# Norms of a two-model block kernel: one VectorE operation per tile, the shift on ScalarE, the order of the backlog around them

## The reference

```
# first model, per layer
mod = silu(c) @ ada_w[i] + ada_b[i]              # shift, scale, gate (one set for x, one for the context)
h = x * (1.0 + scale) + shift
...                                              # layer 0: attention, layer 1: S5
x = layer_norm(alpha * x + gate * ((y * silu(z)) @ w_out[i]), ln_g[i], ln_b[i])

# second model, per layer
hl = rms_norm(xl, norm_mix) * (1.0 + sc1_l) + sh1_l
...                                              # attention, mLSTM, pooling from hl @ w_in
xl = xl + g1_l * (concat @ w_out)
h2l = rms_norm(xl, norm_ffn) * (1.0 + sc2_l) + sh2_l
xl = xl + g2_l * ((silu(h2l @ w_g) * (h2l @ w_u)) @ w_d)
```

## Time and profile before

| | us |
|---|---|
| median of 3 runs | 2583.42 (2580.16 to 2589.23) |
| the profiled execution | 2589.86 |
| its span on the core | 2588.1 |

### The profile page before, as it was taken

The page is one execution under the profiler, slowest core; times in us unless marked ns, Lnnn a source line. Parts: engine busy times, 40 slices in busy tenths (PEclk is TensorE's granted clock), DMA queues, the critical chain, the costliest instruction groups (busy, mean ns, idle before and its releaser), DMA issues.

```text
span 2588.1 us, 33786 instructions
## 1 busy us (share of the span) xinstructions
PE 2212.1 (85%) x13593; PEld 1669.5 (65%) x13593; DVE 1360.2 (53%) x2527; ACT 906.5 (35%) x1779; POOL 504.7 (20%) x457
## 2 busy tenths in 40 slices
PE   6979788869899776489898988779999987977998
PEld 5757566558466565389753444558888855546998
DVE  4548677563446999155443356453333333455554
ACT  3234454551212432154222244232222222344443
POOL 0047878420057950000000011000000000000000
PEclk8989899889899988599898988889999998998999
DMA  8254454643444329975541211332323332315553
GB/s 281 72 176 132 133 149 121 214 132 99 134 107 107 86 67 180 248 205 166 177 124 57 91 57 50 114 100 96 98 88 90 106 109 76 104 49 163 186 164 106
DMA packets 423666, 324.38 MB, mean 125 GB/s; under 512 B 65086, under 2 KB 411470, under 8 KB 422358
## 3 DMA queue, kind: packets, MB, share of 16 engines
q1 hardware_dynamic: 386452, 295.70, 39.2%
q10 hardware_dynamic: 34242, 16.92, 2.3%
q0 software_dynamic: 2816, 9.60, 1.1%
HBM read 292.42 MB, written 29.75 MB: 124 GB/s over the span
## 4 chain that ended last, share of the span: by engine, by line
PE 61%; DVE 13%; POOL 9%; ACT 6%; DMA 5%; issue 4%; SPq 1%; ACTq 1%; DVEq 0%; POOLq 0%
PE ps L119 59%; POOL A L88 8%; ACT A L115 3%; DVE A L88 2%; DMA wbuf<-ctab 2%; DVE R L88 2%; PE ps L122 2%; DVE A L102 2%; DVE A L92 1%; DVE A L105 1%; SPq L125 1%; DVE A L93 1%; DMA wbuf<-in_ada_w 1%; POOL A L125 1%; DVE A L96 1%
## 5 line engine op out<-in xcount | busy, mean ns | idle before, releaser
L119 PE MATMUL ps<-R,R 128*128 128x256 f32 (+1 forms) x3968 | 845.2, 335 | 35.3 <-ACT R L115 25.1
L119 PEld LDWEIGHTS ps<-R,R 128*128 128x128 f32 x3968 | 631.5, 193 | 109.6 <-ACT R L115 30.3
L119 PE MATMUL ps<-HR,R 128*128 128x512 f32 (+1 forms) x1984 | 555.3, 364 | 35.6 <-DVE R L88 24.8
L88 DVE TENSOR_TENSOR R<-wbuf,R 128x1024 fp32r<-128x1024 f32 (+2 forms) x304 | 332.2, 1101 | 376.3 <-ACT R L115 376.1
L115 ACT ACTIVATE A<-ps 128x512 f32<-128x512 f32 (+4 forms) x400 | 210.4, 556 | 613.4 <-PE ps L119 410.1
L119 PEld LDWEIGHTS ps<-HR,R 128*128 128x128 f32 x1984 | 357.1, 193 | 94.4 <-issue 28.6
L88 POOL TENSOR_TENSOR A<-A 128x512 f32<-128x512 f32 (+3 forms) x258 | 294.6, 1156 | 527.0 <-DVE A L96 267.0
L88 DVE TENSOR_TENSOR A<-A 128x128 f32<-128x128 f32 (+4 forms) x796 | 359.6, 482 | 62.8 <-ACT A L115 25.9
L115 ACT ACTIVATE R<-wbuf 128x1024 fp32r<-128x1024 f32 (+2 forms) x304 | 270.0, 894 | 291.1 <-PE ps L119 264.0
L119 PE MATMUL ps<-H,wbuf 128*128 128x512 f32 (+2 forms) x928 | 342.0, 527 | 13.8 <-DVE H L93 13.8
L119 PE MATMUL ps<-A 128*128 128x64 f32 (+10 forms) x1736 | 285.2, 364 | 34.6 <-DMA wbuf<-ctab 9.4
(11 more groups left out here) (102 smaller groups left out, 1624.5 us busy)
## 6 DMA issues: line engine op xcount, KB each, us to landing
wbuf<-in_w_ada SPq DMA_DIRECT2D x48, 1024.0 KB, 5.2
wbuf<-in_ada_w SPq DMA_DIRECT2D x24, 1024.0 KB, 9.7
wbuf<-in_w_out SPq DMA_DIRECT2D x24, 1024.0 KB, 5.6
wbuf<-in_w_ffn_gate SPq DMA_DIRECT2D x22, 1024.0 KB, 5.3
wbuf<-in_w_ffn_up SPq DMA_DIRECT2D x22, 1024.0 KB, 5.7
wbuf<-in_w_ffn_down SPq DMA_DIRECT2D x32, 704.0 KB, 4.7
wbuf<-in_attn_w_in SPq DMA_DIRECT2D x20, 1024.0 KB, 6.8
ctab<-A ACTq DMA_DIRECT2D x64, 256.0 KB, 2.8
```

Source lines behind the costliest of these rows:

```text
L88: return self.op(lambda e: e.tensor_tensor(out, a, b, op))
L119: return self.op(lambda e: e.matmul(out, lhsT, rhs, start=start, stop=stop, skip_group_check=True))
```

## The change

In `LayerNorm` the two operations per k-tile become one scalar_tensor_tensor (X times g times root). For LN1 the beta is folded into `Mod2`: a few small column operations (`columns`) give the shift of H and of alpha times X. For LN2 ScalarE adds beta, in a third piece of the stage, and the backlog steps around it are split 2, 2, 3. In `RmsMod` VectorE does X times column times root, and `act2` adds the shift on ScalarE, behind the square root. For rm2 (`RmsModHalves`) ScalarE writes the high half with the shift, and VectorE makes the low half of k-tile k - 1 behind the root operation of k-tile k; the FFN waits per k-tile. `ffn` gets `prime`: two high halves and one low half of its weights, made before the root, and its two first panels are loaded two backlog panels earlier. In layer 1 the last two backlog steps go ahead of the mixer's output.

```diff
 # Lin3
+    def sp ... if self.prime:
+                    for g in self.grs[0:2]:
+                        load(g)
+                    yield
+    def act ... if self.prime:
+                    for n in (1, 2):
+                        self.act_hi(act, next(ahead))
+                    yield
+    def lows ... if self.prime:
+                    self.make_lo(e, next(ahead), s)
+                    n = 1
+                    yield
 # LayerNorm
                 rsqrt_act(act, self.RS[:, self.c0:512], (self.name, "rs"))
+                yield
+                for k in range(8 if self.bcol else 0):
+                    act.wait_ge(dve_step, (self.name, "g", k))
+                    act.act(X[:, k, self.c0:512], X[:, k, self.c0:512], ACT.Identity, bias=self.bcol(k)
+                            ).then_inc(act_step, (self.name, k))
                 for k in range(8):
-                    dve.tt(X[:, k, c0:512], X[:, k, c0:512], self.RS[:, c0:512], MUL).then_inc(dve_step)
-                    dve.wait_own()
-                    dve.ts(X[:, k, c0:512], X[:, k, c0:512], self.g(k), self.bcol(k), MUL, ADD
-                           ).then_inc(dve_step, (self.name, k))
+                    dve.stt(X[:, k, c0:512], X[:, k, c0:512], self.g(k), self.RS[:, c0:512], MUL, MUL
+                            ).then_inc(dve_step, (self.name, "g", k))
 # Mod2
+            def columns(self, dve):
+                M = MODS[1]
+                dve.wait_ge(act_evac, ("ada1", "t", 7))
+                dve.ts(self.AB, self.B, ALPHA, None, MUL).then_inc(dve_step)
+                for s in range(2):
+                    dve.tt(self.BH[:, s], M[:, 8:16, s], self.B, MUL).then_inc(dve_step)
+                dve.wait_own()
+                for s in range(2):
+                    dve.tt(self.BH[:, s], self.BH[:, s], M[:, 0:8, s], ADD).then_inc(dve_step)
 # flow, LN2
             step(ln)
             step(backlog, 2)
             step(ln)
-            step(backlog, 5)
+            step(backlog, 2)
+            step(ln)
+            step(backlog, 3)
 # RmsMod
             def act2(self, act):
                 rsqrt_act(act, RS[:, self.cc:512], (self.name, "rs"))
+                for k in range(8):
+                    self.shift(act, k)
...
                 for k in range(8):
-                    dve.tt(self.Hd[:, k, cc:512], X[:, k, cc:512], RS[:, cc:512], MUL).then_inc(dve_step)
-                    dve.wait_own()
-                    for s in range(cc // 256, 2):
-                        sl = slice(s * 256, s * 256 + 256)
-                        dve.ts(self.Hd[:, k, sl], self.Hd[:, k, sl], S1[:, k, s:s + 1], MOD[:, self.csh + k, s:s + 1],
-                               MUL, ADD).then_inc(dve_step, (name, k))
+                    for s, sl in self.kinds():
+                        dve.stt(self.Hd[:, k, sl], X[:, k, sl], S1[:, k, s:s + 1], RS[:, sl], MUL, MUL
+                                ).then_inc(dve_step, (name, k))
+                    between(k)
+            def shift(self, act, k):
+                act.wait_ge(dve_step, (self.name, k))
+                for s, sl in self.kinds():
+                    act.act(self.Hd[:, k, sl], self.Hd[:, k, sl], ACT.Identity, bias=MOD[:, self.csh + k, s:s + 1]
+                            ).then_inc(act_step, (self.name, "h", k))
+        class RmsModHalves(RmsMod):
+            def act2(self, act, first):
+                first()
+                rsqrt_act(act, RS[:, self.cc:512], (self.name, "rs"))
+                for k in range(8):
+                    act.wait_ge(dve_step, (self.name, k))
+                    for s, sl in self.kinds():
+                        act.act(HHf[:, k, sl], self.Hd[:, k, sl], ACT.Identity, bias=MOD[:, self.csh + k, s:s + 1]
+                                ).then_inc(act_hi, (self.name, "hi", k))
+            def lo(self, dve, k):
+                dve.wait_ge(act_hi, (self.name, "hi", k))
+                for s, sl in self.kinds():
+                    dve.stt(HLf[:, k, sl], self.Hd[:, k, sl], MOD[:, self.csh + k, s:s + 1], HHf[:, k, sl], ADD, SUB
+                            ).then_inc(dve_lo, (self.name, "lo", k))
 # layer flow
             on(LastHead(1))
-            step(backlog, 2)
+            if l:
+                rest(backlog)
+            else:
+                step(backlog, 2)
             e.mark(N + "mix")
...
             on(rm2)
-            on(second_half(rm2))
-            if l:
-                rest(backlog)
-            else:
-                step(backlog, 4)
+            ff = on(ffn)
             if e.name in ("act", "dve"):
                 e.wait_mark(N + "ff")
-            on(HalvesHT())
-            rest(on(ffn))
+            if e.name == "sp":
+                step(backlog, 2)
+                step(ff)
+                step(backlog, 2)
+            elif e.name == "act":
+                rm2.act2(e, lambda: step(ff))
+            elif e.name == "dve":
+                rm2.dve2(e, lambda: step(ff))
+            if e.name != "sp":
+                step(backlog, 4)
+            rest(ff)
```

More of the change, by code:

```diff
@@ L325, in build, with __init__ @@
         class Lin3:
-            def __init__(self, tiles, GR, gk=8, sub="dve", start=None, lead=0, fine=False):
+            def __init__(self, tiles, GR, gk=8, sub="dve", start=None, lead=0, fine=False, prime=False):
                 self.tiles, self.GR, self.sub, self.start, self.lead, self.fine = tiles, GR, sub, start, lead, fine
+                self.prime = prime
                 self.grs = []
@@ L348, in sp, with load @@
                 done = set()
+                def load(g):
+                    t, k0, kk, k1, nk, pk, width = g
+                    if pk not in done:
+                        done.add(pk)
+                        s = pool_step if self.sub == "pool" else dve_lo
+                        load_panel(sp, pk, t.w, k0, kk, pk[2], width, (s, self.end[pk]))
+                if self.prime:
+                    for g in self.grs[0:2]:
+                        load(g)
+                    yield
                 for j, t0 in enumerate(self.tiles):
                     for t in self.tiles[j:j + 1 + self.lead]:
-                        for _, k0, kk, k1, nk, pk, width in self.groups(t):
-                            if pk not in done:
-                                done.add(pk)
-                                s = pool_step if self.sub == "pool" else dve_lo
-                                load_panel(sp, pk, t.w, k0, kk, pk[2], width, (s, self.end[pk]))
+                        for g in self.groups(t):
+                            load(g)
                     for g in self.groups(t0):
@@ L427, in dve @@
                 lows = self.lows(dve, dve_lo) if self.sub == "dve" else None
+                if self.prime:
+                    next(lows)
+                    yield
                 for j, t in enumerate(self.tiles):
@@ L1189, in flow @@
             step(ln)
+            mod2 = Mod2()
+            if e.name == "dve":
+                mod2.columns(e)
             step(backlog, 4)
-            step(ln)
+            rest(ln)
             step(backlog, 4)
             e.mark("ln1")
-            on(Mod2())
+            on(mod2)
             SS.flow(e, on, backlog)
@@ L2157, in act2, with kinds, dve2 @@
                 rsqrt_act(act, RS[:, self.cc:512], (self.name, "rs"))
+                for k in range(8):
+                    self.shift(act, k)
             def dve(self, dve):
                 pass
-            def dve2(self, dve):
-                cc, name = self.cc, self.name
+            def kinds(self):
+                return [(s, slice(s * 256, s * 256 + 256)) for s in range(self.cc // 256, 2)]
+            def dve2(self, dve, between=lambda k: None):
+                cc, name, rs = self.cc, self.name, RS[:, self.cc:512]
@@ L2164, in dve2 @@
                 dve.wait_ge(mm_done, (name, "ss", 7))
-                rsqrt_dve(dve, RS[:, cc:512], PS[name, "ss"][:, cc:512], D, 1e-6, (name, "rs"))
+                dve.ts(rs, PS[name, "ss"][:, cc:512], 1.0 / D, 1e-6, MUL, ADD).then_inc(dve_evac, (name, "rs"))
+                between(-1)
+                dve.wait_ge(act_step, (name, "rs"))
+                dve.recip(rs, rs).then_inc(dve_step)
+                t = dve.own
                 dve.wait_ge(act_evac, self.mod)
+                S1 = self.S1
@@ new lines, in shift, with dve2, between @@
+            def shift(self, act, k):
[17 more added lines that the diff above has]
+                            ).then_inc(dve_lo, (self.name, "lo", k))
+            def dve2(self, dve, first):
+                def between(k):
+                    if k == -1:
+                        first()
+                    elif k:
+                        self.lo(dve, k - 1)
+                super().dve2(dve, between)
+                self.lo(dve, 7)
@@ L2185, in second_half @@
             return Second()
-        rm1 = RmsMod(N + "m1", 0, VT[:, 224 + 8 * l:232 + 8 * l], 8, 0, x_ready, H, (f"ada{2 + l}", "t", 7))
```

(15 more changed lines are left out.)

40 lines of the change are left out of this document (25 added, 15 removed).

## The result

| | before | after |
|---|---|---|
| median of the runs side by side | 2586.32 us (2580.16 to 2589.3, 4 runs) | 2610.8 us (2608.96 to 2619.09, 4 runs) |
| the profiled execution | 2589.86 | 2608.96 |
| its span on the core | 2588.1 | 2607.1 |
| mean granted clock | 0.914 | 0.909 |

The changed kernel is slower: the ratio is 1.0089, 95% interval 1.0063 to 1.0115. A second comparison, with more runs, gave 1.0070 (1.0045 to 1.0095). By the ratios the change costs 18 to 23 us, and the two profiled executions lie 19.1 us apart. Forecast were +12.2 us and a range up to 2609; the measured median of 2610.8 lies just outside of it. The sign was right and the sum too small.

A forecast was written before the change was run, and what follows sets the result against it. TensorE was taken to carry 61% of the chain, its backlog in lock-step with ScalarE's copies. Seven terms, -4.1 + 0.4 + 6.2 + 6.1 + 7.4 + 3.7 - 7.5 = +12.2, on 2583.4 gave 2595.6 us, range 2577 to 2609.

The forecast's parts named there:

- LN1: First norm, up to S5: eight scalar_tensor_tensor replace eight pairs of VectorE operations; -4.1 us (-3 to -4.3).
- LN2: TensorE waits for the seventh modulation panel, so halved VectorE work gains nothing; ScalarE's shifts delay copies; +0.4 us (0 to +1).
- rm1, layer 0: Backlog copies stand behind ScalarE's 16 shifts, stopping TensorE ahead of Keys; +6.2 us (+4 to +8.5).
- rm1, layer 1: Copies behind ScalarE's shifts again, with two whole backlog products still to do ahead of Keys; +7.4 us (+5 to +9).
- rm2, layer 0: Backlog held behind ScalarE's last shift, fourth backlog panel then loads late, FFN starts later; +6.1 us (+4 to +9).
- end of the mixer, layer 1: Last two backlog steps and a second turn go ahead of the mixer's output halves; +3.7 us (+3 to +4.5).
- rm2, layer 1: No backlog left to block; TensorE starts the FFN on the first low half of H; -7.5 us (-6 to -8.5).
- credit of 1.2 us: Layer 0's rm2: backlog products just done bring back 1.2 us of the FFN first tile's low clock.
- rival C: The forecast's mechanism at lower prices, clock back at once and panel sooner: +3 to +7 us; 12 in 100.
- rival B: Stalls of rm1 are given back later as weights arrive and head norms catch up: 2582.0 us, no change; 10 in 100.
- Rival A: Backlog stays hidden, ScalarE's copies do not hold TensorE for long: -21.5 us, 2561.9 us; 12 in 100.
- rival E: A second pass over two f32 SBUF inputs makes each 256-column operation 0.27 us longer: +26 us, 2621 us; 2 in 100.

The follow-up runs named there:

- experiment that kept TensorE busy: Changed kernel plus eleven 512-column TensorE products nobody reads, ahead of the backlog in rm1 of both layers; 2609.11 us, ratio 1.0054 to the kernel before.
- before again: The kernel before, executed once more without an edit for a second trace; 2584.74 us.
- the first model's norms alone: Kernel before with only the change to LayerNorm, Mod2, LN2's backlog split and the wait of layer 0's rm1 that follows; 2589.55 us, ratio 0.9999.
- rm1's order: Changed kernel with ScalarE doing its three backlog steps ahead of the sixteen shifts in rm1 of both layers; 2589.87 us, ratio 0.9982 to the kernel before.
- both orders: Changed kernel with ScalarE's backlog copies moved ahead in rm1 and between root and high halves in rm2; 2571.71 us, ratio 0.9924; again 2580.93 us, 0.9939.
- the last experiment: ScalarE's order mended in rm1 and rm2, and layer 1's last two backlog steps back in rm2 behind the root; 2569.06 us, ratio 0.9906 to the kernel before.

## Why the prediction was off

Step by step, in the terms of its sum:

| term | forecast | measured |
|---|---|---|
| LN1 | -4.1 | -4.2 (in the other traces with this code -4.2 to -5.7) |
| LN2 | +0.4 | +0.5 (-0.5 to +0.9 in the others) |
| rm1, layer 0 | +6.2 | **+8.7** (+8.8 again) |
| rm1, layer 1 | +7.4 | +7.6 (+7.7) |
| rm2, layer 0 | +6.1 | **+7.9** (+8.1) |
| end of the mixer, layer 1 | +3.7 | +3.5 |
| rm2, layer 1 | -7.5 | -7.0 |
| mixer of layer 1 | none | **+3.1** (+6.1) |
| the other stretches | 0 | -1.0 before LN1, +0.5 in S5, -0.6 elsewhere |
| sum | +12.2 | +19.1 |

**The step that failed is the size of what follows a stop of TensorE.** The sum took the low clock behind the restart to last 4.6 us and let the backlog's products pay a part of it. In rm1 of layer 0 it lasted 8.3 us, and the term of +6.2 measured +8.7; in rm2 of layer 0 the credit of 1.2 us did not come, and with a panel that was later by 0.4 the term of +6.1 measured +7.9. The seven terms add up to +17.0 where +12.2 was forecast. The stretches that the sum put at nothing gave 2 us more in this pair of executions.

**Behind the missed range stands also the base.** The +19.1 of the two profiles would have made 2602.5, which lies within the range. The other 8.3 us up to 2610.8 are the difference between profiles and medians: the forecast took differences within an execution of 2589.86 us and added them to a median of three runs that lies 6.4 us lower, and the profile after lies 1.8 us below its own median. The median of the kernel before was 2586.3 in the comparison side by side and 2593.9, 2589.7 and 2597.4 in the later ones. So the 2583.4 of three runs was itself a term that moves by several us, and the forecast gave it no range.

**The mechanism was right.** ScalarE's `mrow` copies stand behind its shifts and hold TensorE's backlog, and behind that Keys and the FFN. In layer 0, counted from the end of the sum of squares, the copy was forecast 12.5 us behind it and came at 12.4; Keys' first product was forecast at 16.1 and came at 16.6. In layer 1 that was 17.8 and 17.8. In rm2 of layer 0 the copy in question was to end 18.3 us behind the first backlog product and ended at 18.1, the last panel was to be there at 26.1 and was at 26.5, the FFN at 28.3 and was at 29.0. Undoing the order and nothing else took away these three terms and some 10 us more (in rm1 16.1 us in place of the 17.6 of the kernel before, twice, in rm2 12.3 in place of 21.0). The low bound of +4 for rm1, rival C, and rival B, that the stop is given back later, are out: the ratio lies at 0.7 to 0.9%, and the mixer of layer 0 is as long as before to 0.2 us.

**Two terms were too small, mainly by the clock, and one was missing.** First, rm1 of layer 0. The forecast took the low clock to last 4.6 us behind the restart, from the FFN in the earlier trace rows, and so gave Keys' first tile 7.4 us. The granted clock of the kernel after, by windows:

```profile
1312.00:1313.00 1.00, 0.76 (x4) 0.50 0.00 0
1313.00:1315.00 2.00, 2.00 (x18) 0.50 0.04 8
...
1320.00:1321.00 1.00, 1.00 (x3) 0.71 0.02 5
1321.00:1322.00 1.00, 1.00 (x4) 1.00 0.00 0
...
2120.00:2122.00 2.00, 2.00 (x25) 0.50 0.00 0
2122.00:2123.00 1.00, 1.00 (x14) 0.64 0.55 71
```

The clock is the third column from the right. Half clock (1.2 GHz of 2.4) from the restart at 1312.24 until about 1320.6, 8.3 us; the tile took 9.5 us. In layer 1, with one more whole product of the backlog behind the restart at 2118.43, the clock was back at about 2122.7, 4.3 us later, and there the term was right to 0.2. The experiment that kept TensorE busy bears the first reading out: in layer 0, with the clock full throughout, the stretch took 22.39 us in place of 26.28. What made the one twice as long as the other stays open.

Second, rm2 of layer 0. The forecast let the backlog products pay 1.2 us of the low clock ahead of the FFN. They did bring the clock up, and the wait for the panel and the small work behind it took it down again:

```profile
1724.00:1726.00 2.00, 0.00 (x0) 1.00 0.82 288
1726.00:1728.00 2.00, 1.54 (x16) 0.69 0.00 0
1728.00:1730.00 2.00, 2.00 (x11) 0.50 0.03 8
...
1733.00:1734.00 1.00, 1.00 (x5) 0.70 0.66 170
```

The clock was full at 1724 to 1726, with nothing to do, and half again from about 1726.8 to 1733.6; the FFN's first tile started at 1728.97 and took 8.02 us, as in the kernel before. The credit of 1.2 us never came; the other 0.7 is 0.4 at the last panel and 0.3 behind it.

Third, the mixer of layer 1 was not in the sum at all. It has the same instructions in all kernels, and 214.67 to 214.69 us in the three traces with the old rm1 (before, before again, the first model's norms alone). In the nine others it was 216.3 to 224.7: 216.32 with rm1's order, 216.46 and 220.85 in two executions with both orders, 220.28 in the last experiment. The stretches in it that differ are those with a lower clock. One of them, 80 instructions of TensorE (11186 to 11266), by windows: us, busy time of TensorE's products, of its weight loads, of VectorE, ScalarE and GpSimd, the granted clock, the share of the DMA engines, GB/s. In the kernel before:

```profile
2240.21:2253.26 13.05, 10.57 (x83) 6.17 (x86) 8.13 (x22) 7.13 (x22) 1.75 (x4) 1.00 0.22 74
```

In the kernel after:

```profile
2262.04:2278.25 16.21, 13.74 (x82) 7.78 (x85) 8.12 (x22) 7.12 (x22) 1.75 (x4) 0.79 0.17 59
```

In the version with both orders, first execution:

```profile
2224.13:2237.17 13.04, 10.56 (x83) 6.16 (x86) 8.13 (x22) 7.11 (x22) 1.75 (x4) 1.00 0.22 76
```

In the same kernel, sent again:

```profile
2232.00:2248.21 16.21, 13.74 (x82) 7.78 (x85) 8.13 (x22) 7.11 (x22) 1.75 (x4) 0.79 0.18 60
```

The same instructions take 13.05 us at clock 1.00 and 16.21 at 0.79, and the work of VectorE and ScalarE is the same to 0.01. That the lower clock is where the time goes is what the rows show. What brings it on is open. It never came with the old rm1 (three traces) and came in some measure with each new one, which suggests that what runs ahead of the stretch takes part, but no run shows it. One kernel executed twice gave 216.5 and 220.9, and other stretches without an edited operation move as much over the twelve traces: 655.4 to 666.2 us up to LN1's mean, 556.0 to 562.2 in S5, 365.2 to 370.1 in the mixer of layer 0. So a term of 1.6 to 10 us here, and a like one for each long stretch, belongs to the range and not to the sum.

**The sides of the sum that gained came as forecast.** LN1, the two steps at the end of the mixer (3.5 of 3.7, and 3.8 given back when they were moved away), and rm2 of layer 1 each within 0.5 us.

**Rival A had nearly the right price under the wrong order, in part by luck.** It gave 2561.9, 21.5 us below the kernel before, if the backlog stayed hidden. The kernel with both orders, in which ScalarE's shifts no longer hold it, has a profiled span 20.0 below the first profile of the kernel before and 14.8 below the second, and ratios of 0.9924 and 0.9939, 16 to 20 us. Its own terms measured less than they were priced at: 1.4 us in place of 2.2 in each rm1, 7.3 in place of 9.2 in rm2 of layer 0, 17.6 in all. Its condition, less work behind ScalarE's last shift than the norm saves, was broken by the order in the program alone, and an edit of a few lines restores it.

**The range was too tight above.** The highest bounds of its terms add up to +23 (the prediction has +24), and 2609 stands for +25.6. Between the medians side by side the change measured +24.5, which the range would have held; counted from the base of 2583.4 it is +27.4. Of the seven terms only rm1 of layer 0 left its own bounds (+8.7, bound +8.5). What was missing is a bound for the base and one for the long stretches without an edit.

## What to carry to other kernels

When work moves to an engine that also copies small results for another one, list that engine's queue before and after: here sixteen shifts ahead of three copies in rm1, and sixteen high halves ahead of the copies in rm2, turned a gain of 16 to 20 us into a loss of 18 to 23, with every operation as cheap as planned. Put the copies that release another engine's queue ahead of the stream that only keeps pace, and give each such stream its place by what waits behind it. A stop of TensorE costs its own length and then the slower work behind it: the low clock lasted 4.3 to 8.3 us behind the restarts here, and Keys' first tile took 9.5 us in place of 7.4 forecast. Before differences of a few us are read from one profile, the kernel before should be profiled twice: here its two spans were some 5 us apart.

## What the runs showed of the hardware that had not been expected

The low clock behind a restart is not one length: 8.3 us in rm1 of layer 0, 4.3 in rm1 of layer 1 and about 5.1 in rm2 of layer 0 (1718.26 to 1723.4) of the same execution, 4.6 in the earlier trace rows. TensorE was busy by the profile in nearly all of that time.

The clock also fell without a long stop. In the kernel with the extra products it was halved at about 2120.6, behind 10.0 us of unbroken products at full clock, one backlog step and 1.88 us of idleness, and it came back at about 2127.4, with TensorE at work throughout. In rm2 of layer 0 of the kernel after it had been full since about 1723.4, was halved within a microsecond of the restart from 2.83 us of idleness and stayed so until about 1733.6. Extra products followed by only 0.89 us of idleness (layer 0 of the kernel with the extra products) kept it full.

One kernel, executed twice, spent 216.5 and 220.9 us on the same 977 instructions of TensorE; 3.2 us of that lie in the 80 instructions shown above, with the clock at 1.00 and at 0.79. The kernel before spent 214.7 in both of its executions there, but 662.4 and 658.4 up to LN1's mean.

Sixteen scalar_tensor_tensor of 256 columns, all in SBUF and f32, start 0.40 us apart (6.42 us for 16), eight of 512 columns 0.66 apart (5.39 for 8). One of 512 columns takes 0.74 to 0.75 us, against the 0.69 of one tensor_tensor of 512 in the earlier trace rows. The Trainium skill, Vector Engine (DVE) Microarchitecture Reference, section "Points that are easy to get wrong", says that this form runs at half throughput with two SBUF sources that are not bf16. Here it was 0.06 us slower than a tensor_tensor of the same size and not twice as slow, and the 26 us of rival E did not come. Whether both forms run at half of some higher rate no run here shows.
